# RWKV prompt tiles written out instead of looped, and the state chain's parts over half steps 2 to 37

## The chip, the cores and the metric

The kernel runs on one core of a Trainium2 chip. A core has five engines with instruction queues of their own: TensorE (PE; the loading of its weights is listed apart, as PEld), VectorE (DVE), ScalarE (ACT), GpSimd (POOL) and SyncE (SP), which here only issues the weight DMAs. They run side by side and wait for each other with counting semaphores. The metric is the device time of one execution, in microseconds. Before the change its median over 3 runs is 4275.09 us (4273.12 to 4280.93).

## What is computed

One step of a 4-layer decoder with 512 prompt tokens and 8 x 8 sample tokens that share the weights. The layers' mixers are RWKV-7, forgetting attention, a short gated convolution, and RWKV-7 again; each is followed by a convolution FFN. The change touches only the state part of the two RWKV layers. Per head (16 heads of 64) the reference runs over the tokens:

```python
def _wkv_step(S, inp):
    r, k, v, w, kk, b = inp
    sa = jnp.einsum('bhij,bhj->bhi', S, -kk)
    S = S * w[:, :, None, :] + sa[..., None] * b[:, :, None, :] + v[..., None] * k[:, :, None, :]
    return S, jnp.einsum('bhij,bhj->bhi', S, r)
```

`r`, `k` and `v` are projections of the mixed input, `w` is a decay, `kk` the normalised key and `b` is `kk` times a learned rate. Inputs and outputs are fp32.

## The kernel before

The 1024 channels are 8 tiles of 128 (two heads each); the 512 prompt tokens are 8 chunks of 64. For each tile the recurrence is put into the form of triangular 64 x 64 matrices, one per chunk and head. Three kinds of work belong to a tile:

- **preparation** (`prep_*`, 11 pieces): decay sums, exponentials, norms, on DVE, ACT, POOL and a few wide matmuls (L813, L816 for the sample tile, L822, L826). ACT loads a new table for the sigmoid (L882), the square root (L885) and the exponentials (L888).
- **inversion** (`inv_*`, table `INV`, 21 steps with names such as `l`, `lt`, `d2`, `t`, `r2`, `r3`, `r4`): each step is two half steps of 16 small matmuls (L1004) over 8 chunks and 2 heads, and then one copy by ACT (L1018) or one multiplication or addition by DVE (L1028, L1033). The last steps, `r2`, `r3`, `r4`, each need the one before.
- **state chain** (`chain_*`): serial over the 8 chunks of a tile, three parts for each. Part 0 (L1059, L1060) is followed by ACT's copy `a_xb` (L1090), part 1 (L1065 to L1076) needs it and is followed by `a_ust` (L1093), part 2 (L1080, L1083) needs that and is followed by the new state `a_sst` (L1097), which the next chunk's part 0 needs.

`half` issues, in one order for all engines, the inversion of tile c, and in its gaps the chain of tile c - 1 and the preparation of tile c + 1. `CHAIN_AT` gives the half step (of 42) after which each of the 24 chain parts stands, `PREP_AT` the step after which each preparation piece stands. The chain's tile and the tile being prepared share a slot of buffers: the last piece's `ar` (DVE) and `p` (ACT) are written only when the chain no longer reads them. A ninth tile holds the 64 sample tokens of all channels; its inversion has 14 steps (`INV_8`).

`rwkv` (L1124) puts nine halves in a row: tile 0 alone, tiles 1 to 6 in a hardware loop of three turns with two halves each (L1130), then tiles 7 and 8. In the loop, semaphore values and tile addresses are computed from the loop's register (`Bat` with `i`). PE and POOL wait with `hold`, which waits and then increments a semaphore that nobody reads; the other engines use a plain wait.

Of the kernel before, what the change touches and what calls it, by code (L numbers as in the profile page):

```python
# [22 lines left out]
KD = D // P  # L23
# [72 lines left out]
NBAT = KD + 1  # L96
# [18 lines left out]
def build_program(nc, I, O, mixers=MIXERS):  # L115
# [3 lines left out]
    with ctx:  # L119
# [625 lines left out]
        class Bat:  # L745

            def __init__(self, j, c, i=None):
                self.j, self.c, self.i, self.prompt, self.s = j, c, i, c < KD or i is not None, c % 2

            def plus(self, per_tile, v):  # L750

                return v if self.i is None else self.i * (2 * per_tile) + v

            def cnt(self, n, k):

                return self.plus(n, n * (NBAT * self.j + self.c) + k)

            def own(self, which, k):

                n, ns = COUNTS[which]  # L760
                return self.plus(n, (KD * n + ns) * self.j + n * self.c + k)

            def tile(self, n, k):

                return self.plus(n, n * (KD * self.j + self.c) + k)

            def at(self, first):

                return slice(first + self.c, first + self.c + 1) if self.i is None else \
                    bass.ds(self.i * 2 + (first + self.c), 1)  # L770
# [16 lines left out]
        def after(eng, s, v):  # L787

            if not isinstance(v, int) or v > 0:
                eng.wait_ge(s, v)  # L790

        def hold(eng, s, v):

            if not isinstance(v, int) or v > 0:
                eng.wait_ge(s, v)
                eng.sem_inc(s_seen, 1)
# [98 lines left out]
        def prep_pool(pool, B, piece):  # L895
            sl = slots[B.s]
            if piece == 0 and B.prompt:
                hold(pool, a_z, B.cnt(2, 0))
                pool.tensor_copy(w2s[:].unsqueeze(1), lora2[:, 0:D].rearrange("p (k c) -> p k c", c=P)[:, B.at(0)])\
                    .then_inc(a_w2, 1)  # L900
            if piece == 5:
                hold(pool, a_cs, B.cnt(1, 1))
                pool.tensor_tensor(pprev[:, 0], csum[:, 0], zz0, ALU.subtract).then_inc(a_cm, 1)
            if piece == 7:
                hold(pool, a_kk, B.cnt(1, 1))
                pool.tensor_tensor(bb, kraw[:, 0], zz1, ALU.mult).then_inc(a_bb, 1)
            if piece == 8:
                if B.i is not None or B.c > 0:
                    hold(pool, a_m, B.own("m", 1 - COUNTS["m"][0]))
                pool.tensor_copy(sl["v"][:], B.row(rkv, 2 * KD)).then_inc(a_vc, 1)  # L910
            if piece == 9:
                hold(pool, a_bb, B.cnt(1, 1))
                hold(pool, a_ex, B.cnt(3, 1))
                pool.tensor_tensor(sl["bst"][:], bb, pinv[:, 0], ALU.mult).then_inc(a_bk, 1)
                hold(pool, a_kh, B.cnt(2, 2))
                pool.tensor_tensor(sl["kst"][:], kh[:, 0], pinv[:, 0], ALU.mult).then_inc(a_bk, 1)
# [61 lines left out]
        def inv_pe(pe, B, k, part):  # L978
            sl, inv, order = slots[B.s], steps_of(B.prompt), list(steps_of(B.prompt))
            if k >= len(order):  # L980
                return
            name = order[k]
            left, right, bk, _, _, _, needs = inv[name]
            if part == 0:
                if name == "l":
                    hold(pe, a_ar, B.cnt(2, 1))
                    hold(pe, a_bk, B.cnt(2, 1))
                if name == "aak":
                    hold(pe, a_bk, B.cnt(2, 2))
                    hold(pe, a_d, B.own("d", 0))  # L990
                if name == "vst":
                    hold(pe, a_vc, B.cnt(1, 1))
                if name == "p4":
                    hold(pe, a_p1, B.cnt(1, 1))
                if name == "arb":
                    hold(pe, a_ar, B.cnt(2, 2))
                for need in needs:
                    if need in copies_of(B.prompt):
                        hold(pe, a_e, B.own("e", copies_of(B.prompt).index(need) + 1))
                    else:  # L1000
                        hold(pe, a_d, B.own("d", others_of(B.prompt).index(need) + 1))
# [37 lines left out]
        def inv_pool(pool, B, k, part):  # L1039
            sl = slots[B.s]  # L1040
            if k == 1 and part == 1:
                hold(pool, a_d, B.own("d", 1))
                pool.tensor_tensor(sl["m5"][:], sl["m1"][:], mview("ist").unsqueeze(1).to_broadcast([P, NCK, CT]),
                                   ALU.add).then_inc(a_p1, 1)
# [3 lines left out]
        def chain_pe(pe, B, g, part):  # L1048
# [3 lines left out]
            if part == 0:  # L1052
                if g == 0:
                    hold(pe, a_e, B.own("e", COUNTS["e"][0]))
                    hold(pe, a_d, B.own("d", COUNTS["d"][0]))
                hold(pe, a_s, B.tile(NCK, g + 1))
# [5 lines left out]
            if part == 1:  # L1062
                hold(pe, a_xe, n)
# [3 lines left out]
                if g == 0:  # L1067
                    hold(pe, a_oe, B.cnt(1, 1))
# [8 lines left out]
            if part == 2:  # L1077
                hold(pe, a_ue, n)
# [30 lines left out]
        CHAIN_AT = [2 + q * 4 // 3 for q in range(3 * NCK)]  # L1109
# [14 lines left out]
        def rwkv(eng, j, inv_step, chain_part, prep_piece, seq, states_in=None):  # L1124
# [23 lines left out]
        def seq_pe(pe, j, B):  # L1148
            sl = slots[0]
            hold(pe, a_e, B.own("e", COUNTS["e"][1]))  # L1150
            hold(pe, a_d, B.own("d", COUNTS["d"][1]))
            hold(pe, a_out, 16 * (1 + 4 * j))
# [9 lines left out]
            hold(pe, a_qxt, 2 * (j + 1))  # L1162
# [10 lines left out]
            hold(pe, a_qxb, j + 1)  # L1173
# [4 lines left out]
            hold(pe, a_qus, j + 1)  # L1178
# [5 lines left out]
            hold(pe, a_oe, B.cnt(1, 1))  # L1184
            hold(pe, a_bon, B.cnt(1, 1))
            for p in range(KD):
                hold(pe, a_quq, KD * j + p + 1)
                hold(pe, a_qvq, KD * j + p + 1)
                if p >= 2:
                    hold(pe, a_qad, KD * j + p - 1)  # L1190
# [1114 lines left out]
```

## Time and profile before

| what | value |
|---|---|
| runs | 4280.93, 4273.12, 4275.09 us, median 4275.09 |
| profiled execution | 4279.79 us, of it 4277.8 us span |
| mean granted TensorE clock | 0.937 |
| busy | PE 90%, PEld 83%, DVE 41%, ACT 35%, POOL 7% |
| L1004 `m,m` matmuls | x5952, 240.1 us busy |
| DMA | 314.29 MB, mean 73 GB/s |
| instruction DMA | q8 233 packets, 3.82 MB; q14 41 packets, 0.34 MB |

The two RWKV state parts lie at about 268 to 662 us and 3247 to 3640 us. In the rows below, a timeline's line has the start and the length in us, the engine, the line of the code, the operation with its operands, the count, and in brackets the idle time before it and what ended it; "issue" means that nothing the profile shows was waited for. A wait's line has the total in us, how often, and the longest. In a list of windows "(x)" is a count, and the numbers behind are the granted clock (1.00 is 2.4 GHz, 0.50 is 1.2 GHz), the DMA share and GB/s. PEldq is PE's sequencer.

### The profile page before, as it was taken

To read this page: it belongs to the slowest core of one execution; us is meant where nothing else is said; L and a number is where in the kernel's file an instruction comes from. 1 tells how busy PE (TensorE), PEld (TensorE's weight loads), DVE (VectorE), ACT (ScalarE), POOL (GpSimd) and SP (SyncE) were. 2 spreads that over 40 slices of the span, in tenths; PEclk is the share of its full clock that TensorE was granted. 3 is DMA by queue.
4 is the path that set the end of the run, shared out by engine and by line. 5 is a ranking of instruction groups with operands and counts; after the bars stand their busy time and mean duration, and the time that the engine had idled before them with its cause. 6 is when DMAs were issued, how large, how long until landed. Compare 5 with 4: busy or idle time off the path is not lost.

```text
span 4277.8 us, 95379 instructions
## 1 busy us (share of the span) xinstructions
PE 3868.0 (90%) x40189; PEld 3540.0 (83%) x40189; DVE 1772.6 (41%) x2245; ACT 1517.3 (35%) x2377; POOL 283.6 (7%) x556
## 2 busy tenths in 40 slices
PE   6968889899998989889998989999797888989999
PEld 5957775799998975589998989999795768579999
DVE  4364442444326534344423334432546444344432
ACT  2334431244323333334422224432234434124431
POOL 0011211000000000000000000000001211100000
PEclk9979997799999999999999999999897999689999
DMA  3200000122222258622222222223220000012222
GB/s 113 79 21 3 3 22 24 41 74 83 81 85 59 73 190 318 220 65 83 83 82 74 84 66 76 81 81 89 74 73 16 3 3 23 23 46 83 79 82 81
DMA packets 95908, 314.29 MB, mean 73 GB/s; under 512 B 18946, under 2 KB 20226, under 8 KB 94866
## 3 DMA queue, kind: packets, MB, share of 16 engines
q1 hardware_dynamic: 87410, 285.25, 21.1%
q10 hardware_dynamic: 8224, 24.88, 1.5%
q8 instruction: 233, 3.82, 0.4%
q14 instruction: 41, 0.34, 0.0%
HBM read 297.30 MB, written 12.79 MB: 72 GB/s over the span
## 4 chain that ended last, share of the span: by engine, by line
PE 56%; DVE 6%; ACT 3%; issue 2%; DMA 0%; ACTq 0%; DVEq 0%; SPq 0%
PE ps L381 14%; PE ps L383 14%; PE ps L382 14%; PE ps L1004 4%; PE ps L478 1%; DVE xt L686 1%; PE ps L1252 1%; DVE xl L680 1%; DVE xt L401 1%; PE ps L1584 1%; PE ps L813 1%; PE ps L1245 1%; PE ps L1619 1%; PE ps L1639 1%; PE ps L1683 1%
## 5 line engine op out<-in xcount | busy, mean ns | idle before, releaser
L381 PE MATMUL ps<-xh,wh 128*128 128x288 f32 x4976 | 1506.3, 303 | 120.4 <-DVE xl L680 68.3
L382 PE MATMUL ps<-xl,wh 128*128 128x288 f32 x4976 | 1480.8, 298 | 0.0
L383 PE MATMUL ps<-xh,wl 128*128 128x288 f32 x4976 | 1474.7, 296 | 0.0
L365 DVE TENSOR_TENSOR wl<-raw,wh 128x1024 fp32r<-128x1024 f32 x415 | 508.4, 1225 | 1419.1 <-ACT wh L358 1418.7
L381 PEld LDWEIGHTS ps<-xh,wh 128*128 128x128 f32 x4976 | 944.0, 190 | 147.5 <-issue 97.3
L382 PEld LDWEIGHTS ps<-xl,wh 128*128 128x128 f32 x4976 | 947.3, 190 | 2.4
L383 PEld LDWEIGHTS ps<-xh,wl 128*128 128x128 f32 x4976 | 949.3, 191 | 0.0
L358 ACT ACTIVATE wh<-raw 128x1024 fp32r<-128x1024 f32 x415 | 440.4, 1061 | 1428.5 <-PE ps L383 1420.7
L381 PE MATMUL ps<-hh,wh 128*128 128x288 f32 x1536 | 465.3, 303 | 0.0
L383 PE MATMUL ps<-hh,wl 128*128 128x288 f32 x1536 | 456.7, 297 | 0.0
L382 PE MATMUL ps<-hl,wh 128*128 128x288 f32 x1536 | 450.1, 293 | 0.0
L382 PEld LDWEIGHTS ps<-hl,wh 128*128 128x128 f32 x1536 | 294.5, 192 | 2.4
L381 PEld LDWEIGHTS ps<-hh,wh 128*128 128x128 f32 x1536 | 290.7, 189 | 2.7 <-issue 0.2
L383 PEld LDWEIGHTS ps<-hh,wl 128*128 128x128 f32 x1536 | 289.8, 189 | 0.0
L1004 PE MATMUL ps<-m,m 64*64 64x64 f32 x5952 | 240.1, 224 | 33.2 <-DVE m L1033 30.1
L1004 PEld LDWEIGHTS ps<-m,m 64*64 64x64 f32 x5952 | 216.0, 140 | 37.8 <-issue 37.5
L1033 DVE TENSOR_TENSOR m<-ps,m 128x512 f32<-128x512 f32 x100 | 68.8, 688 | 189.8 <-PE ps L1004 187.7
L564 POOL COPY co<-gate 128x2 f32 x96 | 49.9, 520 | 1143.5 <-ACT gate L508 1015.6
L536 DVE TENSOR_TENSOR hf<-conv,ps 128x512 f32<-128x512 f32 x88 | 60.6, 688 | 153.4 <-PE ps L383 153.4
L1090 ACT ACTIVATE a_xb<-ps 128x64 f32<-128x64 f32 x128 | 28.2, 221 | 222.2 <-PE ps L1060 220.2
L514 ACT ACTIVATE conv<-conv 128x592 f32<-128x592 f32 x88 | 61.8, 702 | 119.7 <-DVE conv L531 119.7
L701 ACT ACTIVATE xh<-xt 128x576 fp32r<-128x576 f32 x96 | 66.1, 688 | 106.7 <-DVE xt L686 106.1
(300 smaller groups left out, 4660.9 us busy)
## 6 DMA issues: line engine op xcount, KB each, us to landing
raw<-in_w SPq DMA_DIRECT2D x415, 512.0 KB, 3.5
kp<-in_cache_k SPq DMA_DIRECT2D x64, 512.0 KB, 5.7
vp<-in_cache_v SPq DMA_DIRECT2D x64, 512.0 KB, 5.9
rkv<-in_wkv ACTq DMA_DIRECT2D x2, 2048.0 KB, 9.6
out_wkvs<-rkv ACTq DMA_DIRECT2D x2, 2048.0 KB, 7.2
x<-in_x ACTq DMA_DIRECT2D x1, 2304.0 KB, 13.3
out_k<-qk ACTq DMA_DIRECT2D x1, 2304.0 KB, 7.1
out_v<-vg ACTq DMA_DIRECT2D x1, 2304.0 KB, 12.2
```

What stands on the lines that cost most here:

```text
L358: act.activation(wh[:, c % SPL], raw[:, c % RAWS], ACT.Copy).then_inc(s_hi, 1)
L365: dve.tensor_tensor(wl[:, c % SPL], raw[:, c % RAWS], wh[:, c % SPL].bitcast(F32), ALU.subtract).then_inc(s_lo, 1)
L381: pe.matmul(out, w_h, rhs_h, start=(first and k == 0), stop=False)
L382: pe.matmul(out, w_h, rhs_l, start=False, stop=False)
L383: mm = pe.matmul(out, w_l, rhs_h, start=False, stop=(last and k == nk - 1))
L401: dve.scalar_tensor_tensor(xt[:, k % 2], x[:, k], par[:, col + k:col + k + 1], rstd[:], ALU.mult, ALU.mult).then_inc(s_xt, 1)
L514: act.activation(conv[:, u, 2:GW], conv[:, u, 2:GW], ACT.Silu).then_inc(s_si, 1)
L536: dve.tensor_tensor(tok(hf[:], 0), hist(conv[:, u], 0), tok(pst((n + 1) % 2), 0), ALU.mult)
L564: pool.tensor_copy(co[:, bass.ds(i * 2 + u, 1), 0:2], one(gate[:, u, GS - 2:GS]))
L701: act.activation(xh[:, k], xt[:, k % 2], ACT.Copy).then_inc(s_xh, 1)
L1004: mm = pe.matmul(bank(bk)[r, p * CT:(p + 1) * CT], operand(sl, left, p)[r], mview("ist")[r] if right == "ist" else operand(sl, right, p)[r ...
L1033: dve.tensor_tensor(sl[to][:], src, sl[by][:], ALU.add).then_inc(a_d, 1)
```

## The change

The loop is gone: `rwkv` issues the nine halves one by one, with constants where registers were, so `Bat` loses its index. `hold` is gone: all its uses are now `after`, a wait without the increment. And the 24 chain parts are spread evenly from half step 2 to 37 instead of 2 to 32. What is computed, and each engine's order of inversion and preparation, stay as they are.

```diff
-            def __init__(self, j, c, i=None):
-                self.j, self.c, self.i, self.prompt, self.s = j, c, i, c < KD or i is not None, c % 2
-
-            def plus(self, per_tile, v):
-
-                return v if self.i is None else self.i * (2 * per_tile) + v
+            def __init__(self, j, c):
+                self.j, self.c, self.prompt, self.s = j, c, c < KD, c % 2
...
-        def hold(eng, s, v):
-
-            if not isinstance(v, int) or v > 0:
-                eng.wait_ge(s, v)
-                eng.sem_inc(s_seen, 1)
...
             if part == 1:
-                hold(pe, a_xe, n)
+                after(pe, a_xe, n)
...
-        CHAIN_AT = [2 + q * 4 // 3 for q in range(3 * NCK)]
+        CHAIN_AT = [2 + q * (2 * NSTEP - 7) // (3 * NCK - 1) for q in range(3 * NCK)]
...
-            half(eng, *fns, Bat(j, 0), None, Bat(j, 1))
-            with eng.Fori(0, KD // 2 - 1) as i:
-                half(eng, *fns, Bat(j, 1, i), Bat(j, 0, i), Bat(j, 2, i))
-                half(eng, *fns, Bat(j, 2, i), Bat(j, 1, i), Bat(j, 3, i))
-            if states_in:
-                states_in()
-            half(eng, *fns, Bat(j, KD - 1), Bat(j, KD - 2), Bat(j, KD))
-            half(eng, *fns, Bat(j, KD), Bat(j, KD - 1), None)
+            for c in range(KD + 1):
+                if c == KD - 1 and states_in:
+                    states_in()
+                half(eng, *fns, Bat(j, c), Bat(j, c - 1) if c else None, Bat(j, c + 1) if c < KD else None)
             seq(eng, j, Bat(j, KD))
```

Every other `hold(` in `prep_pool`, `inv_pe`, `inv_pool`, `chain_pe` and `seq_pe` becomes `after(` in the same way.

## Rows read from the trace of the kernel before

**Rows 1.** The page's part 1: busy us, share of the span, instructions.

```profile
PE 3868.0 (90%) x40189; PEld 3540.0 (83%) x40189; DVE 1772.6 (41%) x2245; ACT 1517.3 (35%) x2377; POOL 283.6 (7%) x556
```

**Rows 2.** PEld in order of time, from the end of one tile.

```profile
3332.81 1.04 PEld L1004 LDWEIGHTS ps<-m,m 64*64 64x64 f32 x32 [0.98 <-issue]
3333.74 1.05 PEld L1004 LDWEIGHTS ps<-bst,ar 64*64 64x64 f32 x32
...
3339.30 0.29 PEld L813 LDWEIGHTS ps<-la,w2s 64*128 64x128 f32 x2 [1.57 <-DVE a_zz L836]
```

**Rows 3.** Waits of PE, 3240 to 3650 us.

```profile
PE ps L1065 <- ACT a_xb L1090: 20.9, 22, 1.3
...
PE ps L1004 <- DVE m L1033: 15.0, 17, 1.0
...
PE ps L1004 <- issue: 11.2, 10, 3.6
```

**Rows 4.** The loop's branches by engine, ns min/median/max.

```profile
L1130 PEldq COMPARE_BRANCH  x6: 79/3449/3962, 396.7 to 3563.3; - x6
...
L1130 DVEq COMPARE_BRANCH  x6: 50/56/67, 398.4 to 3564.1; - x6
```

**Rows 5.** PEld after back jumps, and the second L813 loads.

```profile
401.11 1.06 PEld L1004 LDWEIGHTS ps<-bst,ar 64*64 64x64 f32 x18 [3.39 <-issue]
...
3380.15 1.82 PEld L1004 LDWEIGHTS ps<-bst,ar 64*64 64x64 f32 x32 [3.68 <-issue]
...
3388.26 0.29 PEld L813 LDWEIGHTS ps<-la,w2s 64*128 64x128 f32 x2 [1.69 <-DVE a_zz L836]
...
3432.63 0.29 PEld L813 LDWEIGHTS ps<-la,w2s 64*128 64x128 f32 x2 [1.57 <-DVE a_zz L836]
...
3473.87 1.35 PEld L1004 LDWEIGHTS ps<-bst,ar 64*64 64x64 f32 x23 [3.43 <-issue]
```

**Rows 6.** Windows: start of a tile, undisturbed and after a back jump.

```profile
3333.74:3335.90 2.16, 2.16 (x43) 1.34 (x38) 1.62 (x3) 0.00 (x0) 0.07 (x1) 1.00 0.03 8
3380.15:3384.08 3.93, 3.90 (x34) 2.31 (x34) 1.29 (x2) 0.00 (x0) 1.01 (x1) 0.50 0.02 4
```

**Rows 7.** The increments that `hold` issues on PE.

```profile
L796 PEldq EVENT_SEMAPHORE  x925: 51/51/51, 269.8 to 3671.2; - x185
```

**Rows 8.** Timelines of DVE, ACT and PEld at three waits.

```profile
3338.57 0.68 DVE L836 TENSOR_TENSOR a_zz<-ps,par 128x512 f32<-128x512 f32 x1
...
3347.79 0.21 ACT L1090 ACTIVATE a_xb<-ps 128x64 f32<-128x64 f32 x1
...
3348.11 0.22 PEld L1065 LDWEIGHTS ps<-a_xb,m 64*64 64x64 f32 x4 [0.95 <-issue]
...
3582.85 0.22 PEld L1065 LDWEIGHTS ps<-a_xb,m 64*64 64x64 f32 x4 [0.95 <-issue]
```

**Rows 9.** ACT's sigmoid and a table load, PEld's other a_xb stalls.

```profile
3346.82 1.06 ACT L882 ACTIVATE a_zz<-a_zz 128x1024 f32<-128x1024 f32 x1
...
3350.00 1.28 ACT L885 ACT_TABLE_LOAD   x1
...
3352.12 0.22 PEld L1065 LDWEIGHTS ps<-a_xb,m 64*64 64x64 f32 x4 [0.86 <-issue]
...
3360.45 0.22 PEld L1065 LDWEIGHTS ps<-a_xb,m 64*64 64x64 f32 x4 [1.41 <-issue]
```

**Rows 10.** PEld's pauses in the last half, first and last of four.

```profile
3616.10 0.43 PEld L1004 LDWEIGHTS ps<-m,m 64*64 64x64 f32 x12 [1.09 <-issue]
...
3629.22 0.48 PEld L1004 LDWEIGHTS ps<-msk,m 64*64 64x64 f32 x14 [0.54 <-issue]
```

**Rows 11.** A window, and its DMA queue of instructions.

```profile
3290.00:3480.00 190.00, 155.06 (x3905) 134.72 (x3902) 85.79 (x107) 77.35 (x177) 36.37 (x29) 0.93 0.01 3
...
q8 instruction: 34, 0.56, 1.2%
```

**Rows 12.** PEld at the end of the first layer's loop.

```profile
586.51 0.36 PEld L1004 LDWEIGHTS ps<-bst,ar 64*64 64x64 f32 x9 [2.67 <-issue]
```

More of the change, by code:

```diff
@@ L787, in after @@
         def after(eng, s, v):
-            if not isinstance(v, int) or v > 0:
+            if v > 0:
                 eng.wait_ge(s, v)
-        def hold(eng, s, v):
-            if not isinstance(v, int) or v > 0:
-                eng.wait_ge(s, v)
-                eng.sem_inc(s_seen, 1)
         HEADS = [slice(64 * h, 64 * h + 64) for h in range(2)]
@@ L897, in prep_pool @@
             if piece == 0 and B.prompt:
-                hold(pool, a_z, B.cnt(2, 0))
+                after(pool, a_z, B.cnt(2, 0))
                 pool.tensor_copy(w2s[:].unsqueeze(1), lora2[:, 0:D].rearrange("p (k c) -> p k c", c=P)[:, B.at(0)])\
@@ L1041, in inv_pool @@
             if k == 1 and part == 1:
-                hold(pool, a_d, B.own("d", 1))
+                after(pool, a_d, B.own("d", 1))
                 pool.tensor_tensor(sl["m5"][:], sl["m1"][:], mview("ist").unsqueeze(1).to_broadcast([P, NCK, CT]),
@@ L1053, in chain_pe @@
                 if g == 0:
-                    hold(pe, a_e, B.own("e", COUNTS["e"][0]))
-                    hold(pe, a_d, B.own("d", COUNTS["d"][0]))
-                hold(pe, a_s, B.tile(NCK, g + 1))
+                    after(pe, a_e, B.own("e", COUNTS["e"][0]))
+                    after(pe, a_d, B.own("d", COUNTS["d"][0]))
+                after(pe, a_s, B.tile(NCK, g + 1))
                 for r in HEADS:
@@ L1067, in chain_pe @@
                 if g == 0:
-                    hold(pe, a_oe, B.cnt(1, 1))
+                    after(pe, a_oe, B.cnt(1, 1))
                 for r in HEADS:
@@ L1077, in chain_pe @@
             if part == 2:
-                hold(pe, a_ue, n)
+                after(pe, a_ue, n)
                 for r in HEADS:
@@ L1149, in seq_pe @@
             sl = slots[0]
-            hold(pe, a_e, B.own("e", COUNTS["e"][1]))
-            hold(pe, a_d, B.own("d", COUNTS["d"][1]))
-            hold(pe, a_out, 16 * (1 + 4 * j))
+            after(pe, a_e, B.own("e", COUNTS["e"][1]))
+            after(pe, a_d, B.own("d", COUNTS["d"][1]))
+            after(pe, a_out, 16 * (1 + 4 * j))
             for p in range(KD):
@@ L1161, in seq_pe @@
                     mm.then_inc(a_qx, 1)
-            hold(pe, a_qxt, 2 * (j + 1))
+            after(pe, a_qxt, 2 * (j + 1))
             for p in range(KD):
@@ L1172, in seq_pe @@
                               stop=False, skip_group_check=True)
-            hold(pe, a_qxb, j + 1)
+            after(pe, a_qxb, j + 1)
             for p in range(KD):
@@ L1177, in seq_pe @@
             mm.then_inc(a_qU, 1)
-            hold(pe, a_qus, j + 1)
+            after(pe, a_qus, j + 1)
             for p in range(KD):
@@ L1183, in seq_pe @@
             mm.then_inc(a_qo, 1)
-            hold(pe, a_oe, B.cnt(1, 1))
-            hold(pe, a_bon, B.cnt(1, 1))
+            after(pe, a_oe, B.cnt(1, 1))
+            after(pe, a_bon, B.cnt(1, 1))
             for p in range(KD):
-                hold(pe, a_quq, KD * j + p + 1)
-                hold(pe, a_qvq, KD * j + p + 1)
+                after(pe, a_quq, KD * j + p + 1)
+                after(pe, a_qvq, KD * j + p + 1)
                 if p >= 2:
-                    hold(pe, a_qad, KD * j + p - 1)
+                    after(pe, a_qad, KD * j + p - 1)
                 for r in HEADS:
```

41 lines of the change are left out of this document (20 added, 21 removed).

## The prediction

> **What bounds the kernel now.** The page comes first: TensorE (PE) is busy 90% of the span [rows 1], so the question for any edit is what it takes out of PE's time. Then the waits of the two stretches in which the changed code runs, PE's weight loads (PEld) in order of time through a few tiles there, with ACT beside them, and last the loop's own instructions and the granted clock. The RWKV state part runs twice, at about 268 to 662 us and 3247 to 3640 us. Each time it is nine "halves": one tile's inversion (21 steps of 2 x 16 small matmuls), in whose gaps the state chain of the tile before and the preparation of the tile after are placed. In a half without a stall 32 matmuls are issued in 0.93 us (3332.81 to 3333.74 [rows 2]), so a half step of 16 is 0.47 us. At that pace the stream is PE's own. What the change can give back is in the holes.
>
> There are four kinds of holes. (a) At a loop's back jump PE stands for 3.3 to 3.7 us. (b) Three times per half PE waits for ACT's copy of a_xb, and twice for DVE's additions at the end of the inversion: 22 and 17 times in a layer, up to 1.3 and 1.0 us [rows 3]. (c) Waits that hang on DVE in the preparation, which no edit touches. (d) Short pauses in the middle of a dense run, with nothing to wait for; with two of the back jumps they are the 11.2 us of "issue" in front of L1004 in one layer [rows 3].
>
> **1. The loops written out.** Only PE suffers from the loop: its compare-and-branch takes 79 ns where it falls through and a median of 3449 ns, at most 3962, over all six; DVE's takes 50 to 67 [rows 4]. The four PE back jumps show as 3.39, 3.27, 3.68 and 3.43 us of idle time at the first matmuls of the next half [rows 5] (rows 5 show all but the second), where the same place without a jump shows none (3333.74 [rows 2]). Sum: 13.8 us, all on the path, as PE alone sets the pace there.
>
> The pause also costs clock. Right after it the granted clock is 0.50, the 1.2 GHz level, and 34 matmuls take 3.93 us; at the same place of the half before it is 1.00 (2.4 GHz) and 43 take 2.16 us [rows 6]. From the half's first load to the second L813 is 5.56 us undisturbed (3333.74 to 3339.30 [rows 2]) and 8.11 us after a jump (3380.15 to 3388.26 [rows 5]): 2.55 us more, four times, 10.2 us. Top: 13.8 + 10.2 = 24.0 us. A second way, by whole halves between the second L813s: 48.96 us with a jump (3339.30 to 3388.26) and 44.37 without (to 3432.63) [rows 2, 5], 4.6 us each, 18.4 us; here the half without a jump has more pauses of kind (d), and after two of the jumps the clock is low for longer. I take 24, with 18 as the low end; nothing suggests more than 28.
>
> The Trainium skill ("Advanced Engine Details and Errata", Control Flow Timing) gives a compare-and-branch about 108 ns; by it four jumps would be 0.4 us. DVE's rows fit that order of size, PE's do not. The same page (ISA Cache) speaks of blocks of 16 KB or 256 instructions and of few of them held. That would explain the difference, but no row here measures the cache.
>
> The register arithmetic of the loops goes too. It costs nothing now: the first stall for a_xb is 0.95 us of idle weight load inside the loop and again in the half behind it, which has no registers (3348.11 and 3582.85 [rows 8]). The other three engines get more code, which they must fetch once. I price that at nothing: they are idle most of a half, and if it leaked it would show as more waiting for ACT or DVE on PE.
>
> **2. `hold` becomes `after`.** 925 semaphore increments of 51 ns leave PE's sequencer [rows 7], and POOL's the same way. All on the path, PE's would be 47 us. But in a dense run the sequencer is ahead of the array, and matmuls pass the hold at their usual pace. Only where PE really waits does it count. With hold: a_xb ends at 3347.79 + 0.21 = 3348.00 and the load starts at 3348.11, 0.11 us later. With the wait on the matmul itself: L836 ends at 3338.57 + 0.68 = 3339.25 and the load starts at 3339.30, 0.05 us later [rows 2, 8]. So 0.06 us per real wait. Of rows 3, 22 + 17 per layer, 78 in both: 4.7 us; bounds 0 (the wait stays an instruction of its own) and 8 us. I take 4.5. Two waits in a row, as before the first matmul of a tile, stay one separate instruction and one on the matmul.
>
> **3. The chain's 24 parts over half steps 2 to 37.** Before: 2, 3, 4, 6, 7, 8, ... 30, 31, 32, the three parts of a chunk always adjacent. After: 2, 3, 5; 6, 8, 9; 11, 12, 14; 15, 17, 18; 20, 21, 23; 24, 26, 27; 29, 30, 32; 33, 35, 37. Nothing is added; part 0 is 0.23 us of PE, part 1 is 0.58, part 2 is 0.23. What moves is where ACT's work on the chain falls against its three table loads (1.28 us each), which are what a_xb waits behind now: 0.95, 0.86 and 1.41 us of idle weight load in one half [rows 8, 9]. By the order of each engine's queue:
> - Sigmoid (after half step 9), 1.28 + 1.06. Before, a_xb follows at once. After, the copy of a step (0.60) gets in between, but PE has one more half step and part 0 (0.70) before it needs a_xb. The stall stays at about 1.0 us.
> - Square root (after 13), 1.28 + 0.60. Before, 0.97 us of stall, issue to issue. After, ACT starts the table load while PE still has 13 and 14 to do, and what waits is the next chunk's part 0, for the state copy (0.32): about 0.58. Gain 0.4.
> - Exponentials (after 21), 1.28 + 0.63 + 0.48. The state copy of half step 23 now sits behind them and a step's copy: 1.64 against 1.50. Loss 0.14.
> - Where part 2 and the next part 0 are now adjacent (5 to 6, 14 to 15, 32 to 33), the state's round trip of 0.37 + 0.32 + 0.05 meets 0.70 us of PE work: 0.04 each, 0.12.
> - Half step 37 falls into the hole before the next step, where PE waits for DVE: 0.23 us are now free.
>
> Per half: -0.4 + 0.14 + 0.12 - 0.23 = -0.37, of which 0.1 is already in part 2's sum; times 14 halves, -4 us. At the end of each pass the last half has only 28 half steps, so more of the chain runs bare: one and a half chunks instead of a half. A bare chunk costs about 1.2 us beyond its own work: +2.4 us for both passes. Net -1.5; bounds -8 (all three table stalls shrink) and +8, if half step 37 delays DVE's `ar` writes, which wait for the whole chain and for ACT's last exponential. By the queues they end 0.04 us before DVE's next addition is due; a miss of 0.6 us in each of 14 halves makes the 8.
>
> **4. The pauses of kind (d).** In the last half, straight code already, they come every 4.4 us: 1.09, two between, 0.54, in all 2.3 us [rows 10]. 34 instruction packets serve 3905 + 3902 loads and matmuls in 190 us [rows 11], so a packet is used up in about 3.7 us of dense running, and a pause comes where none of the stalls lies in between. They total some 8 us now: in one layer 11.2 us less two back jumps of 3.5 [rows 3, 5], twice. Fewer instructions in the stream, and waits that no longer hold the sequencer, speak for less; a denser stream speaks for more. I take -1.5, from -6 to +8. One more pause is a matter of luck: at the end of layer 0's loop PE stood 2.67 us at 586.51 while, as the table of DMA issues has it, the 2 MB of `rkv<-in_wkv` were on their way [rows 12]; in the other layer nothing. With its clock loss that is some 5 us, which can stay, go or come twice. I leave it where it is.
>
> **Sum.** 24 + 4.5 + 1.5 + 1.5 = 31.5 us. The profiled execution took 4279.8 us (span 4277.8, 2.0 around it), so 4248.3; it stands 4.7 above the median of the runs, 4275.1, so **4243.6 us** as a median.
>
> **Rivals.**
> - *The fetch comes back as pauses* (12%). The back jump's 3.3 to 3.7 us are spread over straight code. For it: rows 10 show straight code pausing. Against: the half behind the loop, just as dense, has no idle entry of that kind. Time: gain 24 + 4.5 less another 15, 4262.
> - *The chain's spacing and the freed sequencer pay more than I count* (11%). For it: the three table stalls make up 3.5 us of every half. Against: the sigmoid's is set by ACT, whatever PE does. Gain 43, 4232.
> - *Slower: straight code is starved* (4%). The two passes take some 8 packets a half [rows 11], 14 halves, 110 packets. Break-even is 31.5 / 110 = 0.29 us more of pause per packet. At the 0.57 us average of the last half [rows 10] everywhere, less the 8 us there are now, it is 110 x 0.57 - 8 = +55: 4275 - 31 + 55 = 4299. Against it: inside a loop's body the code is straight too, and the pauses there are few.
> - *The loops never cost anything net* (2%): the branch is cheap, the pause at the jump is a wait the profile does not name and stays. Time 4275 - 6 = 4269 or unchanged. By the skill's 108 ns this would be the likeliest. Against: only the jumps taken show the pause.
>
> **How the numbers follow.** My forecast has 71% and by itself runs from 4236 to 4253. The range has to take in the parts' bounds and the near halves of the first two rivals: 4232 to 4259. A measurement of this kernel tells 0.2%, 8.5 us. All cases but the starved one and half of the fourth are faster by more than that: faster 0.94, within 0.02, slower 0.04.
>
> **What would show it.** PE's branches of L1130 and the register instructions gone; no PE idle over 3 us inside either pass; clock at 1.00 in the windows of tiles 3 and 5; the second L813s 43 to 44 us apart in all tiles; 0.05 instead of 0.11 us from a_xb's end to L1065; one a_xb stall per half instead of three, and two new waits for a_sst at L1059. Wrong would be: new idle entries of 0.5 to 1 us every 4 us (rival one or three), a wait for `ar` or `p` at the end of the half (part 3), or a changed time outside the two stretches.

## The result, and the profile after

The changed kernel takes 4208.05 us (median of 4 runs, 4199.44 to 4215.91), the kernel before 4277.9 us in the same comparison (4 runs, 4273.12 to 4280.93). The ratio is 0.9834, with a 95% interval of 0.9818 to 0.9849. That is 70 us less, where 31.5 were forecast. It is faster, as forecast, but 24 us below the lower end of the range. Run once more beside the kernel before (e15), it gained 62.8 us (4273.41 to 4210.60).

The page's part 1: PE's busy time fell by 41 us and its share hardly moved against [rows 1], DVE's busy time rose by 21 us.

```profile
PE 3826.8 (91%) x40189; PEld 3504.9 (83%) x40189; DVE 1793.6 (43%) x2245; ACT 1512.9 (36%) x2377; POOL 287.1 (7%) x556
```

All but 1.5 us of the gain lies in the two passes of the state part. In this text a pass runs from the first matmul of its inversion to the first matmul of the sample tokens' sequences. Before, the passes took 391.3 and 388.2 us, after 355.7 and 355.6: 68.2 us of the 69.7 between the two profiled executions. Here are the windows of both passes, set within 0.4 us of their ends. The columns are the window, its length, then busy us and count of PE, PEld, DVE, ACT and POOL, the granted clock, the DMA share and GB/s. First the kernel before:

```profile
270.40:661.40 391.00, 324.45 (x8124) 284.92 (x8122) 173.15 (x215) 157.63 (x357) 69.53 (x55) 0.91 0.03 8
3249.20:3637.40 388.20, 322.25 (x8124) 283.31 (x8125) 173.02 (x216) 157.94 (x359) 69.63 (x56) 0.92 0.03 8
```

and the changed kernel:

```profile
272.70:628.40 355.70, 303.53 (x8125) 268.69 (x8127) 182.79 (x216) 156.40 (x357) 70.94 (x55) 0.95 0.03 9
3211.50:3567.20 355.70, 303.50 (x8125) 268.73 (x8127) 182.86 (x216) 156.28 (x357) 70.96 (x55) 0.95 0.03 9
```

The window's length less PE's busy time is PE's idle time. Over both passes it fell from 132.5 to 104.4 us, by 28.1, where the forecast had 21.3 in its sum. The other 39.7 us came out of PE's **busy** time (646.7 to 607.0), with the same matmuls (8124 a pass); there the forecast had 10.2. The granted clock gives a part of it: 0.91 and 0.92 before, 0.95 after. By the trace's record of the clock, PE was busy at 0.50 for 113 us of the passes before and for 62 after. Taken at half pace, that is 26 of the 39.7 us (an estimate). The other 14 are matmuls that follow each other more closely at the full clock; e1 and e3 below show where.

The order of time shows the steps. The start and the length in us stand first. Between the last loads of a tile (from 3293.49) and the first of the next (3294.42) there is no idle time at any tile, where four had 3.3 to 3.7 us [rows 5]. (L802 is the line that was L813 before.)

```profile
3293.49 1.01 PEld L993 LDWEIGHTS ps<-m,m 64*64 64x64 f32 x32 [1.06 <-DVE m L1022]
3294.42 1.02 PEld L993 LDWEIGHTS ps<-bst,ar 64*64 64x64 f32 x32
...
3299.81 0.29 PEld L802 LDWEIGHTS ps<-la,w2s 64*128 64x128 f32 x2 [1.70 <-DVE a_zz L825]
...
3339.80 0.29 PEld L802 LDWEIGHTS ps<-la,w2s 64*128 64x128 f32 x2 [1.71 <-DVE a_zz L825]
...
3381.26 0.29 PEld L802 LDWEIGHTS ps<-la,w2s 64*128 64x128 f32 x2 [1.71 <-DVE a_zz L825]
...
3421.26 0.29 PEld L802 LDWEIGHTS ps<-la,w2s 64*128 64x128 f32 x2 [1.70 <-DVE a_zz L825]
```

The second L802 loads are 39.99, 41.46 and 40.00 us apart, where 48.96 and 44.37 stood before [rows 2, 5] and 43 to 44 were forecast. In the windows below the first line is a tile's start, the place where [rows 6] had 0.50 after a back jump; the second and third lines are two tiles as a whole. The tile of 41.46 has a spell of low clock behind its L802: the last two lines are its first 6.8 us.

```profile
3294.42:3296.58 2.16, 2.16 (x44) 1.33 (x40) 1.65 (x3) 0.00 (x0) 0.19 (x1) 1.00 0.03 8
...
3299.81:3339.80 39.99, 34.23 (x957) 30.13 (x957) 22.01 (x26) 19.09 (x44) 8.90 (x7) 1.00 0.01 3
3339.80:3381.26 41.46, 35.70 (x956) 31.45 (x956) 22.00 (x26) 19.10 (x44) 8.90 (x7) 0.96 0.02 4
...
3339.80:3343.20 3.40, 3.40 (x44) 2.50 (x46) 0.19 (x1) 0.00 (x0) 0.00 (x0) 0.62 0.02 5
3343.20:3346.60 3.40, 3.40 (x104) 3.38 (x101) 1.10 (x2) 1.42 (x5) 0.00 (x0) 0.87 0.00 0
```

PE's waits in the second pass and some us around it (total, how often, longest), against [rows 3]:

```profile
PE ps L815 <- DVE a_zz L852: 18.6, 9, 11.2
PE ps L993 <- DVE m L1022: 13.1, 17, 1.2
PE ps L1048 <- ACT a_sst L1086: 12.1, 17, 1.3
PE ps L802 <- DVE a_zz L825: 11.4, 7, 2.0
PE ps L1054 <- ACT a_xb L1079: 5.9, 9, 0.7
```

The a_xb waits fell from 22 to 9 and from 20.9 to 5.9 us, and 17 waits for the state a_sst stand where there was one of 0.4 us. No "issue" is left in front of L993, where 11.2 us stood. The 11.2 us maximum of L815 lies before the first inversion and was there already (10.2); without it L815's waits for DVE rose from 4.3 us to 7.4, with kh's length in DVE (e12 to e16) a possible cause. The table of branches has no PE line of `rwkv` any more, and the 925 increments of [rows 7] are gone.

One a_xb stall and the two new a_sst stalls, by order of time:

```profile
3308.61 0.21 ACT L1079 ACTIVATE a_xb<-ps 128x64 f32<-128x64 f32 x1
3308.88 0.19 PEld L1054 LDWEIGHTS ps<-a_xb,m 64*64 64x64 f32 x4 [0.88 <-ACT a_xb L1079]
...
3311.64 0.20 PEld L1048 LDWEIGHTS ps<-a_sst,ar 64*64 64x64 f32 x4 [0.43 <-ACT a_sst L1086]
...
3319.64 0.20 PEld L1048 LDWEIGHTS ps<-a_sst,ar 64*64 64x64 f32 x4 [1.46 <-ACT a_sst L1086]
```

From a_xb's end (3308.82) to the load it is now 0.06 us, where it was 0.11 [rows 8]. Issue to issue the three stalls are 1.02, 0.56 and 1.60 us. Of [rows 9] the two that answer to the square root and the exponentials are gone, and these two a_sst stalls stand in their place. In the last half (3542 to 3567 us), where [rows 10] had pauses of 1.09 and 0.54 us, no idle entry over 0.2 us is put down to issue, and near 587 us, where [rows 12] had 2.67, nothing stands. The instruction queue is no busier: 35 packets serve 4467 matmuls in 190 us, against 34 for 3905 [rows 11].

```profile
3255.00:3445.00 190.00, 163.01 (x4467) 143.51 (x4465) 103.48 (x122) 91.09 (x208) 42.66 (x34) 0.98 0.01 3
...
q8 instruction: 35, 0.57, 1.3%
```

### The profile page after: what moved, and what is told of

Its sections match the earlier page's. It is cut to its first block, busy times and chain, and to the rows that moved or that the text cites. A ratio compares the mean times of both kernels' runs of the same rounds, so it can differ in the third digit from the quotient of the medians.

```text
span 4208.2 us, 93473 instructions
## 1 busy us (share of the span) xinstructions
PE 3826.8 (91%) x40189; PEld 3504.9 (83%) x40189; DVE 1793.6 (43%) x2245; ACT 1512.9 (36%) x2377; POOL 287.1 (7%) x556
## 4 chain that ended last, share of the span: by engine, by line
PE 56%; DVE 6%; ACT 4%; issue 1%; DMA 0%; ACTq 0%; SPq 0%; DVEq 0%
PE ps L381 14%; PE ps L383 14%; PE ps L382 14%; PE ps L993 3%; PE ps L478 1%; DVE xt L686 1%; PE ps L1237 1%; DVE xl L680 1%; DVE xt L401 1%; PE ps L1569 1%; PE ps L1230 1%; PE ps L1604 1%; PE ps L1624 1%; PE ps L1668 1%; PE ps L802 0%
## 5 line engine op out<-in xcount | busy, mean ns | idle before, releaser
L993 PE MATMUL ps<-m,m 64*64 64x64 f32 x5952 | 228.5, 222 | 27.3 <-DVE m L1022 26.2
L993 PEld LDWEIGHTS ps<-m,m 64*64 64x64 f32 x5952 | 207.1, 139 | 32.2 <-DVE m L1022 28.2
L1022 DVE TENSOR_TENSOR m<-ps,m 128x512 f32<-128x512 f32 x100 | 68.7, 687 | 165.7 <-PE ps L993 165.6
L1007 ACT ACTIVATE m<-ps 128x512 f32<-128x512 f32 x120 | 71.1, 595 | 81.1 <-PE ps L993 81.1
## 6 DMA issues: line engine op xcount, KB each, us to landing
rkv<-in_wkv ACTq DMA_DIRECT2D x2, 2048.0 KB, 10.1
```

Source lines behind the costliest of these rows:

```text
L1007: act.activation(flat(sl[to][:]), bank(bk), ACT.Copy).then_inc(a_e, 1)
L1022: dve.tensor_tensor(sl[to][:], src, sl[by][:], ALU.add).then_inc(a_d, 1)
```

## The experiments

"Straight" means the loops written out, "old places" half steps 2 to 32 for the chain, "new places" 2 to 37. e1 to e16 were run in four comparisons of four kernels each, and each ratio is to the kernel before in the same comparison (medians 4273.29, 4274.84, 4272.91 and 4273.41).

| kernel | median us | ratio [95%] | passes us |
|---|---|---|---|
| changed kernel | 4208.05 | 0.9834 [0.9818, 0.9849] | 355.7 / 355.6 |
| e1 straight, hold, old | 4235.86 | 0.9913 [0.9896, 0.9930] | 369.1 / 369.8 |
| e2 straight, hold, new | 4224.78 | 0.9881 [0.9864, 0.9897] | 365.1 / 364.0 |
| e3 straight, after, old | 4208.92 | 0.9847 [0.9831, 0.9864] | 354.9 / 354.9 |
| e4 loop, hold, new | 4261.98 | 0.9968 [0.9955, 0.9980] | 383.3 / 380.7 |
| e5 increment first, old | 4206.86 | 0.9836 [0.9820, 0.9853] | 355.5 / 355.6 |
| e6 wait twice, old | 4216.04 | 0.9860 [0.9843, 0.9876] | 361.8 / 362.4 |
| e7 one back jump | 4255.23 | 0.9951 [0.9934, 0.9967] | 378.1 / 376.2 |
| e8 places by ACT | 4236.59 | 0.9905 [0.9889, 0.9922] | 370.2 / 370.8 |
| e9 the same, pieces 8, 9 later | 4247.74 | 0.9937 [0.9920, 0.9953] | 376.9 / 376.1 |
| e10 pieces 8, 9 later, old | 4229.74 | 0.9899 [0.9882, 0.9915] | 366.3 / 365.9 |
| e11 pieces 8, 9 later, new | 4216.27 | 0.9867 [0.9851, 0.9884] | 358.6 / 358.9 |
| e12 POOL keeps hold, old | 4197.01 | 0.9819 [0.9803, 0.9835] | 353.2 / 355.1 |
| e13 POOL keeps hold, new | 4199.41 | 0.9826 [0.9810, 0.9841] | 350.3 / 353.5 |
| e14 bb behind kh, new | 4200.11 | 0.9820 [0.9804, 0.9835] | 353.7 / 354.0 |
| e15 changed kernel again | 4210.60 | 0.9846 [0.9830, 0.9863] | 355.7 / 355.7 |
| e16 bb behind kh, old | 4210.24 | 0.9853 [0.9836, 0.9871] | 355.7 / 357.5 |

The passes are the sharper measure: those of the changed kernel came out the same within 0.1 us in both its profiled executions (e15 is the second). The span less the passes runs from 3486 us (e12) to 3502 (e15), though most of it is code that no experiment touched, so a few us between two kernels' times can come from there.

### The three parts, alone and in steps (e1 to e4)

e1: only the loops are written out, from the kernel before.

```diff
-            with eng.Fori(0, KD // 2 - 1) as i:
-                half(eng, *fns, Bat(j, 1, i), Bat(j, 0, i), Bat(j, 2, i))
...
+            for c in range(KD + 1):
```

> Only the loops are written out; hold and the old chain places stay. Theory A (the pauses of kind (d) come from hold: PE's sequencer stands at each held wait and so reaches the next block of instructions late): the back jumps and their clock loss go, some 24 to 30 us, the pauses in dense runs stay at about 9 to 13 us per pass; time 4248 to 4254. Theory B (the pauses come from the loop, which empties what was fetched): they go here already, gain 45 us or more, 4233 or less. Theory C (spacing): as A.

e2: e1 with the new places.

```diff
-        CHAIN_AT = [2 + q * 4 // 3 for q in range(3 * NCK)]
+        CHAIN_AT = [2 + q * (2 * NSTEP - 7) // (3 * NCK - 1) for q in range(3 * NCK)]
```

> Loops written out and the new chain places, hold stays: the whole change but for hold. Theory A: pauses stay, gain 24 to 34 us, 4244 to 4254. Theory C (the even spacing breaks the dense runs in which the pauses arise): pauses go, gain 60 us or more.

e3: e1 with `after` for `hold`, on PE and POOL (the changed kernel with e2's edit undone).

```diff
-                hold(pe, a_xe, n)
+                after(pe, a_xe, n)
```

> Loops written out and after in place of hold, the old chain places: the whole change but for the spacing. Theory A: pauses gone (under 3 us per pass), gain 58 to 66 us, 4212 to 4220. Theory C: pauses stay, gain some 30 us.

e4: the kernel before with e2's edit alone.

> Only the new chain places; loops and hold stay. By the recorded working of the spacing alone (three table stalls 3.5 to 3.2 us, 0.23 us hidden, longer tail): gain 0 to 4 us, 4274 to 4278. Theory C: gain 20 us or more. The back jumps of 3.3 to 3.9 us are all there.

The passes of e1 (loops gone, hold kept):

```profile
270.10:639.40 369.30, 311.87 (x8127) 276.24 (x8128) 174.29 (x216) 157.07 (x358) 69.63 (x55) 0.95 0.03 9
3225.30:3595.20 369.90, 312.91 (x8125) 277.07 (x8126) 174.62 (x216) 157.10 (x359) 69.72 (x56) 0.95 0.03 9
```

of e3 (hold gone too):

```profile
272.60:627.70 355.10, 300.15 (x8128) 266.30 (x8130) 184.12 (x217) 155.54 (x357) 70.93 (x55) 0.97 0.03 9
3215.00:3570.00 355.00, 300.07 (x8128) 266.20 (x8128) 184.12 (x217) 155.43 (x357) 70.96 (x55) 0.97 0.03 9
```

and of e4 (only the places):

```profile
269.80:653.30 383.50, 324.32 (x8129) 285.96 (x8130) 171.85 (x216) 156.74 (x359) 69.16 (x56) 0.90 0.03 8
3242.90:3623.70 380.80, 320.82 (x8126) 282.83 (x8127) 171.68 (x216) 156.83 (x357) 69.58 (x55) 0.92 0.03 9
```

Length less PE busy, and PE busy, over both passes of each step:

| step | idle | busy | sum |
|---|---|---|---|
| loops out (before to e1) | -18.1 | -21.9 | -40.0 |
| hold out (e1 to e3) | -4.5 | -24.6 | -29.1 |
| new places, without hold (e3 to changed) | -5.5 | +6.8 | +1.3 |
| new places, with hold and loop (before to e4) | -13.3 | -1.6 | -14.9 |

The first two steps carry the whole gain, and the larger part of both is busy time. From before to e1 that is clock: PE was busy at 0.50 for 113 us before and for 66 in e1. From e1 to e3 it is 66 to 40, about half of the 24.6; the rest follows with e5 and e6. The new places are worth 11 us while hold is there, with the loop (4273.3 to 4262.0) and without (4235.9 to 4224.8), and nothing that can be measured once it is gone (4208.9 against 4208.05 and 4210.6). They do take idle time out, but the granted clock gives it back: 0.97 in e3, 0.95 in the changed kernel, where three tiles of a pass have the spell shown above. The medians of the parts don't add up: 37 + 27 + 11 would be 75.

### What a back jump costs (e7)

The loop runs two turns instead of three, with one tile more ahead of it on each pass, so there is one PE back jump per pass instead of two.

```diff
+            half(eng, *fns, Bat(j, 1), Bat(j, 0), Bat(j, 2))
+            half(eng, *fns, Bat(j, 2), Bat(j, 1), Bat(j, 3))
-            with eng.Fori(0, KD // 2 - 1) as i:
...
+            with eng.Fori(0, KD // 2 - 2) as i:
+                half(eng, *fns, Bat(j, 3, i), Bat(j, 2, i), Bat(j, 4, i))
+                half(eng, *fns, Bat(j, 4, i), Bat(j, 3, i), Bat(j, 5, i))
```

> Hold and the old chain places; tiles 1 and 2 written out, tiles 3 to 6 in a loop of two turns: one back jump per pass instead of two. If each back jump costs the same (idle time plus the clock that stays low behind it), half of the 37 us comes back: 4252 to 4258, and one stretch of low clock behind the jump in each pass. If the cost hangs on having a loop at all: near 4273 or near 4236.

e7's branches on PE's sequencer, ns min/median/max: two fall through and two jump.

```profile
L1132 PEldq COMPARE_BRANCH  x4: 79/1908/3926, 485.0 to 3541.0; - x4
```

4274.84 to 4255.23 us: 19.6 us for two of the four jumps, and e1 takes 37.4 for four. So a jump costs 9 to 10 us, not the 6.0 of the forecast. 3.3 to 3.7 of it is the stop. The rest is behind it: taken spell by spell, the clock was at 0.50 behind the four jumps for 17.1, 13.7, 10.2 and 17.1 us. In the passes it was there for 129 us before (70.5 and 58.6) and for 70 in e1. The forecast compared with an undisturbed tile only up to the second L813, 8 us behind the jump, and there the spell was half over.

Why PE stops at these jumps is not shown, but not every back jump does it. PE's back jumps in the kernel's other loops, with bodies of 190 to 580 matmuls, took 0.21 to 0.24 us, where the body of two tiles has 1912 and took 3.3 to 4.0. One of them, in the kernel before:

```profile
L621 PEldq COMPARE_BRANCH  x50: 76/208/226, 882.8 to 4115.6; - x50
```

That fits instructions that must be fetched anew when the body is too long to be kept, but no run changed the length of a body.

### What in hold costs (e5, e6)

e5 swaps its two instructions; e6 waits a second time in place of the increment. Both are e1 otherwise.

```diff
-                eng.wait_ge(s, v)
-                eng.sem_inc(s_seen, 1)
+                eng.sem_inc(s_seen, 1)
+                eng.wait_ge(s, v)
```

> Straight code, old chain places; the increment is issued, but ahead of the wait, so that the wait rides on the matmul. Same number of instructions as with hold. Theory A (what costs is that PE's sequencer stands at a wait of its own): as with after, 4209 to 4215. Theory D (the increments themselves cost, as instructions to fetch and issue): as with hold, about 4236.

```diff
-                eng.sem_inc(s_seen, 1)
+                eng.wait_ge(s, v)
```

> Straight code, old chain places; the same wait is written twice and nothing is incremented, so that one of the two is an instruction of its own. Theory A: the cost of hold is all there, 4230 to 4240. Theory D: near after, 4209 to 4215, since there is no increment.

e5's increments on PE's sequencer are as many and as long as before [rows 7], and the first pass's waits of e6 for a_xb are as many:

```profile
L795 PEldq EVENT_SEMAPHORE  x925: 51/51/51, 267.0 to 3598.6; - x185
```

```profile
PE ps L1065 <- ACT a_xb L1090: 21.0, 22, 1.3
PE ps L1004 <- DVE m L1033: 15.3, 17, 1.3
```

In the trace of the kernel before and of e1, each of the 925 is one instruction of PE's sequencer that waits and increments, and the load behind it carries no wait. In e5 and e3 the wait rides on the load: 2159 of PE's loads carry one, where 1425 did. e5 has all 925 increments and none of hold's cost (4206.86, e3 4208.92; the passes 355.5 to 354.9). So the 47 us of increments are free, as forecast, and what costs is that the wait is not on the load but on an instruction of its own. In e6 PE has 784 instructions that only wait, and the loads wait once more. It costs 7 us against e3, 14.4 in the passes; hold costs 27, and 29.1 in the passes. (e6 doubles POOL's waits as well; against e12, the kernel whose POOL behaves alike, it is 15.9 in the passes.)

```profile
269.60:631.40 361.80, 306.75 (x8125) 272.08 (x8125) 174.38 (x216) 157.17 (x357) 70.41 (x55) 0.96 0.03 9
```

The forecast looked for this at the 78 waits that stop PE, 0.06 us each. e1 and e3 issue the same 8124 matmuls a pass in the same order, so their starts can be laid side by side. Of the 28.6 us that e1 has more up to the last of them, 5.6 lie at stops: 10.2 more at 121 places where PE is idle in either kernel, 0.08 us each, less 4.6 at two where e3 waits longer for DVE (L852). 11.5 lie between matmuls without a stop at clock 1.00, of them 10.4 just before the 781 matmuls that stand behind a hold or a wait, 13 ns each. And 11.6 lie in spells of 0.50. e6 has 0.4, 8.7 and 5.1 in the same three parts, and e5 has none over 1 us. Why hold is twice as dear as a bare wait stays open; in e6 the load behind carries a wait of its own, in hold it doesn't.

### Moving the work (e8 to e11)

From the changed kernel, tries to lay the chain around ACT's table loads, and to bring piece 8, whose wide matmul L815 waits for DVE's L852, to a later step. e8 (its sample tile's half has places of its own, 2 to 28):

```diff
-        CHAIN_AT = [2 + q * (2 * NSTEP - 7) // (3 * NCK - 1) for q in range(3 * NCK)]
-        PREP_AT = {0: 0, 1: 1, 3: 2, 4: 3, 6: 4, 8: 5, 10: 6, 12: 7, 14: 8, 16: 9, 18: 10}
+        CHAIN_AT = [2, 3, 4, 6, 7, 8, 9, 10, 13, 14, 18, 20, 21, 22, 23, 25, 29, 30, 31, 33, 34, 35, 36, 37]
+        PREP_AT = {0: 0, 1: 1, 3: 2, 4: 3, 6: 4, 8: 5, 11: 6, 12: 7, 14: 8, 16: 9, 18: 10}
```

> The changed kernel, but with the chain parts placed by ACT's queue: 2, 3, 4; 6, 7, 8; 9, 10, 13; 14, 18, 20; 21, 22, 23; 25, 29, 30; 31, 33, 34; 35, 36, 37, the exponentials (piece 6) after step 11 instead of 10, and in the sample tile's half all parts within half steps 2 to 28. By the queues the three table stalls of 1.0, 0.56 and 1.6 us a half shrink to about 0.6 in all. If they are net cost: 14 halves by 2.5 us, 35 us, 4170 to 4180 and better than 4208. If PE only trades them for other waits (DVE's results, the pauses): 4195 to 4210.

e9 (the chain as in e8; only ACT's part of piece 6 stays at 11):

```diff
+        PREP_AT = {0: 0, 1: 1, 3: 2, 4: 3, 6: 4, 8: 5, 10: 6, 12: 7, 16: 8, 17: 9, 18: 10}
+        PREP_ACT = {(11 if k == 10 else k): piece for k, piece in PREP_AT.items()}
```

> As e8_places_by_act, but with preparation pieces 8 and 9 after steps 16 and 17 instead of 14 and 16, and only ACT's exponentials moved by a step. In e8 the three ACT stalls fell from 27 to 10.5 us a pass, and the wait of piece 8's matmul (L815 of the changed kernel) for DVE's L852 rose from 9 to 29 us. If DVE is simply late for a matmul that could come later, the wait falls to 5 us or less and the pass to 340 us: 4175 to 4185. If DVE's own work (182 us busy of 356) is now what paces the half, the wait turns up at the next thing DVE owes and the time stays above 4205.

e10 and e11: e9's `PREP_AT` alone, in e3 and in the changed kernel.

> Straight code, after, the old chain places, pieces 8 and 9 after steps 16 and 17. Takes away the 10 us a pass of the L852 wait if nothing else waits for DVE there: 4190 to 4195; unchanged at 4209 if the time only moves into another wait.

> The changed kernel with pieces 8 and 9 after steps 16 and 17. As e10, 4189 to 4196, if spacing and this wait are independent; more than e10 if the new places give DVE less time.

All four were slower than the kernels they came from. PE's waits in e8's first pass:

```profile
PE ps L815 <- DVE a_zz L852: 27.6, 8, 4.9
PE ps L993 <- DVE m L1022: 13.1, 17, 1.2
...
PE ps L1054 <- ACT a_xb L1079: 1.4, 7, 0.2
```

and in e10's:

```profile
PE ps L993 <- DVE m L1022: 28.3, 25, 5.4
PE ps L1054 <- ACT a_xb L1079: 18.9, 22, 1.2
```

In e8 the a_xb waits are gone, as meant (5.9 to 1.4 us), and the a_sst waits with them, but PE reaches L815 earlier, and DVE has the multiplication L852 ready no sooner. In e10 the wait at L815 is gone, but PE waits 25 times for the inversion's additions L1022 instead of 17. In order of time, DVE's part of piece 9 (L855) now stands right in front of one of them:

```profile
353.95 0.68 DVE L855 TENSOR_TENSOR rkv<-ps,rkv 128x512 f32<-128x512 f32 x1
354.55 0.68 DVE L1022 TENSOR_TENSOR m<-ps,m 128x512 f32<-128x512 f32 x1
...
355.28 1.01 PEld L993 LDWEIGHTS ps<-m,m 64*64 64x64 f32 x32 [1.19 <-DVE m L1022]
```

DVE's queue through the preparation is what is late next, whichever wait is removed. But idle time is the smaller half of what e8 lost. Its first pass:

```profile
272.60:642.80 370.20, 313.21 (x8126) 275.43 (x8126) 192.61 (x216) 154.48 (x359) 70.72 (x56) 0.92 0.03 9
```

Against the changed kernel the two passes have 9.6 us more idle time and 20.0 us more busy time, at 0.92 instead of 0.95. In e10 against e3 it is 12.2 and 9.9, at 0.95 instead of 0.97. Longer single stops (3.5 us each at L815 in e8, where the changed kernel has 0.9) went along with a lower clock here.

### POOL and DVE side by side (e12 to e16)

e12 is e3 with `hold` for POOL's waits alone (the line below and seven others); e13 is the same with the new places.

```diff
-                after(pool, a_kk, B.cnt(1, 1))
+                hold(pool, a_kk, B.cnt(1, 1))
```

> Straight code, old chain places; PE waits with after, POOL keeps hold. If the 27 us of hold are PE's, as e5 and e6 suggest: 4207 to 4212. If POOL's increments delay what PE waits for (POOL is on the way from the scan to the exponentials): up to 4236.

> The changed kernel, but POOL keeps hold (wait and increment); PE waits as in the changed kernel, places 2 to 37. Question: does POOL's hold really pay, as the 12 us between the two kernels with the old places suggested (their intervals overlap)? Theory O, the overlap of POOL and DVE costs: with POOL's plain wait its multiplication bb and DVE's kh start within 0.02 us of each other, POOL first, and kh takes 1.79 us instead of 0.69, 8 times a pass. With the hold kh is back at 0.69 and POOL's takes 1.74. Expected 4198, ratio to the changed kernel 0.9975. Theory N, covered: behind kh DVE waits 0.79 us for PE anyway, so its length is hidden, and what one profile showed was spread over the whole span: within 4 us of the changed kernel of this call. I hold N likelier, 60 to 40.

e14 (from the changed kernel) and e16 (from e3) put POOL's bb behind DVE's kh by its wait; e15 is the changed kernel.

```diff
             if piece == 7:
-                after(pool, a_kk, B.cnt(1, 1))
+                after(pool, a_kh, B.cnt(2, 2))
```

> The changed kernel, but POOL's bb waits for DVE's kh (one instruction later) instead of for the normalised key, so that the two can't start together. Both theories: kh 0.69 us and bb 1.27 us in the trace, unless bb now meets the next DVE multiplication. Theory O: 1.1 us of DVE less, 8 times a pass, at least half of it on the path: 4198. Theory N: no change, 4204 to 4212, and the wait of PE for the bonus multiplication (L852, 9 us a pass) stays.

> The changed kernel itself, so that the other three are read against it on the same chip. Expected 4208 (4203 to 4213) by both theories.

> No loop, no hold at all, old places 2 to 32, and POOL's bb waits for DVE's kh. Theory O: as the kernel with POOL's hold at the old places, 4197. Theory N: as the kernel without it, 4209.

The two instructions, ns min/median/max, in the changed kernel (DVE's kh, POOL's bb):

```profile
L847 DVE SCALAR_TENSOR_TENSOR a_kn<-a_zz,rkv x18: 1779/1791/1795, 264.7 to 3525.7; 128x512 f32<-128x512 f32 x18
L895 POOL TENSOR_TENSOR a_zz<-a_kraw,a_zz x18: 1260/1267/1270, 264.6 to 3525.7; 128x512 f32<-128x512 f32 x18
```

in e12:

```profile
L853 DVE SCALAR_TENSOR_TENSOR a_kn<-a_zz,rkv x18: 692/693/694, 265.0 to 3517.3; 128x512 f32<-128x512 f32 x18
L901 POOL TENSOR_TENSOR a_zz<-a_kraw,a_zz x18: 1738/1744/1750, 265.0 to 3517.3; 128x512 f32<-128x512 f32 x18
```

in e14:

```profile
L847 DVE SCALAR_TENSOR_TENSOR a_kn<-a_zz,rkv x18: 691/692/694, 264.7 to 3522.3; 128x512 f32<-128x512 f32 x18
L895 POOL TENSOR_TENSOR a_zz<-a_kraw,a_zz x18: 1261/1263/1767, 265.4 to 3523.1; 128x512 f32<-128x512 f32 x18
```

So a plain wait on POOL made DVE's instruction 2.6 times as long, and either edit brings it back. On the path this is worth less than it looks. Windows from the first inversion matmul of the first layer to the next wide stage, of e15, e13 and e14:

```profile
270.40:749.80 479.40, 416.46 (x8770) 330.57 (x8771) 228.87 (x275) 173.63 (x384) 89.39 (x71) 0.87 0.04 12
```

```profile
271.70:741.60 469.90, 408.39 (x8770) 323.04 (x8771) 219.72 (x275) 173.40 (x384) 87.95 (x71) 0.88 0.04 12
```

```profile
271.30:745.10 473.80, 410.33 (x8770) 326.05 (x8771) 221.43 (x275) 173.40 (x384) 85.70 (x72) 0.88 0.04 12
```

DVE is 9.2 and 7.4 us less busy there. PE's idle time (length less busy) is 62.9, 61.5 and 63.5 us, the same within 2 us: theory N is right that DVE's length is covered. But the times came out as theory O had them, for PE's busy time is 8.1 and 6.1 us less, at a higher clock. Both e13 and e14 beat e15 (4199.4 and 4200.1 against 4210.6; the runs, 4194 to 4203 and 4192 to 4203 against 4202 to 4215, barely touch). About half of that lies behind the passes, in the sample tokens' stage, where kh and bb don't run: 123.7 us twice in e15, 119.6 and 119.9 in e13, 120.1 and 119.8 in e14. With the old places bb behind kh does nothing (e16 4210.2, theory N's time). POOL's hold seems to help there (e12 4197.0 to e3's 4208.9, intervals of the ratios overlapping), but the passes give only 1.5 us of it. Here is the stage behind the first pass, of e3 and of e12:

```profile
627.60:748.80 121.20, 110.20 (x655) 59.35 (x650) 46.09 (x59) 17.01 (x27) 18.41 (x16) 0.64 0.06 21
```

```profile
625.10:741.80 116.70, 105.56 (x652) 55.77 (x647) 46.09 (x59) 17.01 (x27) 18.42 (x16) 0.66 0.06 21
```

Both stages give 5.4 us, and over half of the 14.5 us between the two profiled executions lies in code that is the same in both. That the overlap lengthens DVE's instruction is shown; that undoing it makes the kernel faster is borne out at the new places alone, and why it moves the clock there is not shown.

The fastest kernels are e12, e13 and e14, 8 to 14 us under the changed one by the medians and not told apart from each other.

## Why the prediction was right or wrong

**What bounds the kernel.** Right: PE's stream in the two passes, holes and clock. What failed is that the holes were counted, the clock at one place only, and the pace of the matmuls between them not at all.

**Step 1, loops, 24 us: the mechanism right, the size wrong.** Measured 37.4 (e1), 40.0 in the passes. The idle part, forecast 13.8, was 18.1, with the pause of [rows 12], left in the sum, going too. The clock's part was mis-sized: 10.2 forecast, 21.9 measured, because the windows ended 8 us behind the jump and the clock stayed low for 10 to 17. The second way by whole halves gave less still (4.6 us a jump), because the half that it compared with had low clock (0.96 as a whole), the tail of the spell behind the same jump, and pauses too. The other engines' code cost nothing, as forecast.

**Step 2, hold, 4.5 us with 8 as the upper bound: this is the step that failed.** Measured 27 for both engines, 29.1 in the passes, and 30.6 in the passes for PE's alone (e1 to e12; 39 by the medians, the rest outside the passes). The 0.05 us from a_xb's end to the load came as forecast (0.06), and the idle time fell by 4.5, with 6.5 more in front of L852 against it. But "in a dense run the sequencer is ahead of the array, and matmuls pass the hold at their usual pace" is what e1, e3 and e5 refute: with hold, 781 matmuls at the waits start 13 ns later though PE doesn't stop (10.4 us), 121 stops are longer by 0.08 us each (10.2 us), and the spells of low clock take 11.6 us more. It is not the increments, it is the wait that is not on the load.

**Step 3, places, 1.5 us.** Each of the three stalls came in its place and size (1.0, 0.58 and 1.64 forecast; 1.02, 0.56 and 1.60 measured), the a_xb stalls fell from three to one, and the order r2 to r3 gained (0.82 us between them instead of 1.12). The net in the final kernel, 1.5 us longer in the passes and between 1 us less and 2 us more by the medians, is 3 us short of the forecast's gain of 1.5 and within its bounds. What the forecast did not see is that it nets so little because the clock takes back idle time (5.5 us less idle, 6.8 more busy), and that with hold it was worth 11.

**Step 4, pauses, 1.5 us of some 8.** The sign is right, the size was too small. PE's idle time put to issue in the passes, the back jumps left out, was 10.1 us before (the 2.5 of [rows 12] among them), 5.8 in e1 and nothing in e3 and the changed kernel. So all of it went, the larger part with hold. It did not hang on how much is fetched: the instruction queue's packets per matmul hardly changed. The forecast's 3.7 us for a packet of dense running is not what its rows give: 7807 loads and matmuls in 34 packets are 115 matmuls each, 3.4 us at 0.029. No term of the sum used it.

**The rivals.** "The fetch comes back" and "starved" are refuted by the absent issue entries, "the loops never cost anything" by e1 (37.4 us). The nearest was "the chain's spacing and the freed sequencer pay more": its second half is what happened, but at 43 us it was priced by the table stalls, which did not matter. The Trainium skill's compare-and-branch figure ("Advanced Engine Details and Errata", Control Flow Timing: about 108 ns) does not hold for PE here: 79 ns where it falls through, 0.21 to 0.24 us where it jumps in a short loop, 3.3 to 4.0 in the loop of two tiles, and there 10 us in all by e7. The chances given for a faster kernel add up to 0.95 with half of the fourth case, not 0.94.

**The range.** Its lower end took both errors at a fraction of their size. Steps 1 and 2 missed by 13 to 16 and by 22 to 25 us, together 36 to 41. That is what lies between the forecast's gain and the measured one (31.5 to 69.9, or 62.8 in e15).

## What to carry to other kernels

Where PE's stream is made of small matmuls, price a stop by the whole spell of low clock behind it, read in windows that go on until the clock is at 1.00 again, and compare busy time as well as idle time: with the same matmuls, 39.7 of 67.8 us came out of "busy". Let a wait ride on the load or matmul that needs it and put nothing between them; an increment that must stay goes ahead of the wait. Compare two kernels of the same order matmul by matmul: it shows whether time went at stops, between them, or to the clock. Before a wait is made cheaper on a side engine, look at what its instruction will start beside.

## What the runs showed of the hardware

- A taken back jump of PE in a loop body of two tiles (1912 matmuls) took 3.3 to 4.0 us, with 10 to 17 us at 0.50 behind it; in loop bodies of 190 to 580 matmuls of the same kernel it took 0.21 to 0.24 us. On DVE the branch of the long loop took 50 to 67 ns.
- PE's waits on an instruction that also increments, 925 of them, cost 30.6 us in the passes (e1 to e12); the same increments ahead of waits that ride on the loads cost nothing (e5).
- Of two elementwise instructions of DVE and POOL on SBUF started within 0.1 us, the one that starts first keeps its time and the other is stretched: kh 1.79 and bb 1.27 us with POOL 0.025 us ahead (e3 and the changed kernel), kh 0.69 and bb 1.74 with DVE 0.075 us ahead (before, e12, e13), at all 18 places. Apart they take 0.69 and 1.26 (e14). The Trainium skill ("GPSIMD Engine Reference", Specifications) says that the two engines share their way into SBUF and that a DVE instruction with two SBUF inputs contends for it; these rows agree, as kh has two.
- The same PE work (8770 matmuls) was 408 to 416 us busy in e13, e14 and e15 with idle time equal within 2 us. The difference went along with the granted clock (0.87 to 0.88); what moved the clock, no run here shows.
